# One level of Strassen's algorithm in the last stage of a hybrid encoder block

## The reference

```
n = rmsnorm(x, g1);  proj = n @ w_in              # 1024 -> 2048: q, k, v, u
att = rmsnorm(diff_attention(q, k, v), g_sub)     # 4 heads, width 512
ssm = bi_s5_glu(u)                                # width 512
h = x + concat(att, ssm) @ w_out                  # 1024 x 1024
h = h + square(relu(rmsnorm(h, g2) @ w_mlp1)) @ w_mlp2   # 1024 -> 4096 -> 1024
y = rmsnorm(h, g_final)
```

## Time and profile before

| | us |
|---|---|
| median of 3 runs | 2963.97 (2961.86 to 2968.33) |
| the profiled execution | 2968.97 |
| its span, first to last instruction | 2967.4 |
| PE busy / DVE busy / ACT busy / POOL busy | 2770.5 / 1709.1 / 1207.5 / 360.5 |
| matmuls on PE | 13768 |
| DMA | 322.47 MB, mean 109 GB/s |
| `phase_mlp`, its first instruction to the end | 1309.9 to 2967.4 |

### The profile page before, as it was taken

One profiled execution on the slowest core, in us unless ns is written; L12 is line 12 of the kernel. 1 busy time (PEld: TensorE's weight loads), 2 busy tenths in 40 slices (PEclk: granted clock), 3 DMA queues, 4 the chain that ended last, 5 costly groups with the idle time before them and its releaser, 6 DMA issues.

```text
span 2967.4 us, 37703 instructions
## 1 busy us (share of the span) xinstructions
PE 2770.5 (93%) x13768; PEld 2331.9 (79%) x13768; DVE 1709.1 (58%) x2380; ACT 1207.5 (41%) x1864; POOL 360.5 (12%) x300
## 2 busy tenths in 40 slices
PE   6978796999999979879999999999999999999996
PEld 5756585999999967767888878888788888788885
DVE  7665517999999947755434365343554343743434
ACT  3365514878787732233324223233233242332331
POOL 5220001101010013303000131000230001400001
PEclk9989898999999989989999999999999999999998
DMA  5335524020220049734232334322252322332222
GB/s 168 139 144 204 182 73 112 22 65 24 65 72 22 17 125 268 189 142 145 96 99 93 98 101 164 99 93 99 91 173 92 99 92 99 100 125 93 99 93 70
DMA packets 160986, 322.47 MB, mean 109 GB/s; under 512 B 30160, under 2 KB 87760, under 8 KB 157136
## 3 DMA queue, kind: packets, MB, share of 16 engines
q1 hardware_dynamic: 143568, 265.58, 29.1%
q10 hardware_dynamic: 10368, 29.89, 2.7%
q0 software_dynamic: 6912, 25.17, 2.3%
HBM read 255.05 MB, written 63.44 MB: 107 GB/s over the span
## 4 chain that ended last, share of the span: by engine, by line
PE 49%; DVE 3%; DMA 1%; issue 1%; POOL 0%; ACT 0%; DVEq 0%; POOLq 0%; ACTq 0%
PE ml_work L2130 9%; PE ml_work L2131 8%; PE ml_work L2132 8%; PE ml_down L2130 8%; PE ml_down L2132 8%; PE ml_down L2131 8%; DMA ml_x_in<-in_x_t 1%; DVE ml_w_lo L1805 1%; PE ml_spread L2093 0%; DVE ml_hg_lo L1946 0%; DVE ml_h L1942 0%; DVE ml_h_out L1931 0%; DMA ml_mix<-att_s 0%; DVE ml_h_out L2017 0%; DVE ml_square L2028 0%
## 5 line engine op out<-in xcount | busy, mean ns | idle before, releaser
L1805 DVE TENSOR_TENSOR ml_w_lo<-ml_w_raw,ml_w_hi 128x1024 fp32r<-128x1024 f32 x288 | 368.4, 1279 | 795.5 <-ACT ml_w_hi L1801 795.3
L1801 ACT ACTIVATE ml_w_hi<-ml_w_raw 128x1024 fp32r<-128x1024 f32 x288 | 305.5, 1061 | 1032.9 <-PE ml_down L2132 542.0
L2130 PE MATMUL ml_work<-ml_hg_hi,ml_w_hi 128*128 128x512 f32 x1024 | 399.4, 390 | 0.8 <-DVE ml_w_lo L1805 0.6
L2130 PE MATMUL ml_down<-ml_act_hi,ml_w_hi 128*128 128x512 f32 x1024 | 399.0, 390 | 0.0
L2132 PE MATMUL ml_work<-ml_hg_hi,ml_w_lo 128*128 128x512 f32 x1024 | 398.5, 389 | 0.0
L2132 PE MATMUL ml_down<-ml_act_hi,ml_w_lo 128*128 128x512 f32 x1024 | 398.4, 389 | 0.0
L2131 PE MATMUL ml_work<-ml_hg_lo,ml_w_hi 128*128 128x512 f32 x1024 | 398.4, 389 | 0.0
L2131 PE MATMUL ml_down<-ml_act_lo,ml_w_hi 128*128 128x512 f32 x1024 | 398.4, 389 | 0.0
L886 ACT ACTIVATE at_e<-at_e,at_neg_top 128x2048 f32<-128x2048 f32 x128 | 256.6, 2005 | 38.1 <-DVE at_neg_top L971 38.1
L1081 PEld LDWEIGHTS at_pv<-at_v,at_a_t 128*128 128x128 f32 x2048 | 259.0, 192 | 16.4
L1081 PE MATMUL at_pv<-at_v,at_a_t 128*128 128x128 f32 x2048 | 260.3, 276 | 0.0
(11 more groups left out here) (221 smaller groups left out, 4409.5 us busy)
## 6 DMA issues: line engine op xcount, KB each, us to landing
ml_w_raw<-in_w_stream SPq DMA_DIRECT2D x290, 512.0 KB, 3.5
tab_s<-pj_tab ACTq DMA_DIRECT2D x32, 512.0 KB, 2.6
pj_x_raw<-in_x_t SPq DMA_DIRECT2D x14, 1024.0 KB, 8.2
ss_tab<-tab_s SPq DMA_DIRECT2D x17, 512.0 KB, 13.7
pj_w_raw<-in_w_in SPq DMA_DIRECT2D x16, 512.0 KB, 4.0
qk_s<-pj_qku_out SPq DMA_DIRECT2D x32, 256.0 KB, 2.5
at_k_raw<-qk_s SPq DMA_DIRECT2D x16, 512.0 KB, 7.5
at_q_raw<-qk_s SPq DMA_DIRECT2D x128, 64.0 KB, 2.4
```

What stands on the lines that cost most here:

```text
L1801: act.activation(w_hi[:, r % 2], w_raw[:, (r + 2) % RAW], ACT.Copy).then_inc(w_hi_ready, 1)
L1805: dve.tensor_tensor(w_lo[:, r % 2], w_raw[:, (r + 2) % RAW], w_hi[:, r % 2].bitcast(F32), ALU.subtract)\
L2130: pe.matmul(out, lhs_hi, rhs_hi, start=first, stop=False)
```

## The change

`phase_mlp` is written anew. Each matrix product of 1024x1024 weights with 1024x1024 activations (a chunk) is split into 2x2 quarters of 512x512 and computed by Winograd's form of Strassen's algorithm: seven products of quarters (steps) instead of eight, with four sums of weight quarters (S1 to S4) and four of activation quarters (T1 to T4). There are 18 chunks: `MIX` for the two halves of 1024 tokens, then for each half four `UP` and four `DOWN`. A step is 4 output tiles (`slot`) by 4 k-tiles by the same three matmuls of 128x512. A quarter lies in a tile of 128x2048, so every split, sum and evacuation is one instruction of 2048 columns.

Two PSUM tiles of four banks alternate from step to step. The products that several results share are summed in PSUM: step 0's tile is copied to the other (`copy_over`, ACT, a quarter at a time), and later steps add to what a tile holds. After steps 1 to 6 the tile is added to a result `res` by DVE (`leave`), or in UP after steps 1, 2, 3 and 6 taken by ACT, which also applies Relu and Square. The split of step g+1 is made while step g is computed; DVE first evacuates step g-1.

Weights and activations are loaded by SP in quarters of 1 MB (`load_r`, `load_q`), the activations from memory: the relu-squares of UP (`act_s`), h (`h_s`) and the normalized h (`hn_s`) are stored there, from ACT's queue (`store_res`) and SP's. When h or y of a half is complete (after chunks 0, 1, 9 and 17; `event`), POOL sums its squares (`add_squares`, 14 adds), PE sums them over partitions with a matrix of ones (`statistics`, 128x512), ACT takes the root, DVE inverts 128x512 twice (`invert`) and multiplies 16 tiles of 128x512 (`normalize`), which SP reads back into two buffers `hb` and stores (`load_hb`, `store_hb`), during steps 0 to 4 of the next chunk. After the last chunk this is done at once, out of `res`.

The scaling and transposing of attention's output move into the gate loop of `phase_ssm`, one head's tile per item, two items behind: `att_scale` (DVE), `turn_att` (PE), `att_back` (ACT), `store_att` (SP). The 4 MB are loaded after `y_done`.

```diff
 # phase_ssm
+            sp.wait_ge(y_done, NGR)
+            for i in range(2):
+                for tb in range(2 * i, 2 * i + 2):
+                    sp.dma_start(att_in[:, tb], att_s.rearrange("h p t -> p h t")[:, :, tb * TB:(tb + 1) * TB])\
+                        .then_inc(att_loaded[i], 16)
...
+            def att_back(n):
+                act.wait_ge(att_turned, n + 1)
+                wait(act, att_stored[n % 2], 16 * (n // 2))
+                act.activation(att_out[:, n % 2], turn_ps[:, n % 2], ACT.Copy, scale=gain_att[:, 0:1]).then_inc(att_ready, 1)
...
+            act.wait_ge(total_step, 1)
+            act.activation(total[:], total[:], ACT.Sqrt).then_inc(total_step, 1)
...
+            def att_scale(n):
+                tb, c = n // H, n % H
+                if n in (0, 2 * H):
+                    dve.wait_ge(att_loaded[tb // 2], 32)
+                rows = att_in[:, tb, c].rearrange("p (c e) -> p c e", c=NC)
+                dve.tensor_tensor(rows, rows, total[:, c, tb * NC:(tb + 1) * NC].unsqueeze(2).to_broadcast([P, NC, P]),
+                                  ALU.mult).then_inc(att_scaled, 1)
...
+                for c in range(NC):
+                    last = pe.transpose(turn_ps[:, n % 2, c * P:(c + 1) * P], att_in[:, n // H, n % H, c * P:(c + 1) * P], ident[:])
+                last.then_inc(att_turned, 1)
             pe.wait_ge(glu_loaded, 32)
...
 # phase_mlp
-def phase_mlp(nc, x_t, att_s, att_square, att_floor, ssm_s, w_stream, gains, y_t):
...
+def phase_mlp(nc, x_t, att_t, ssm_s, h_s, hn_s, act_s, w_stream, gains, y_t, hb_stored):
...
+    MIX, UP, DOWN = 0, 1, 2
+    CHUNKS = [(MIX, 0, 0), (MIX, 1, 0)]
+    for s_ in range(2):
+        CHUNKS += [(UP, s_, c) for c in range(4)] + [(DOWN, s_, c) for c in range(4)]
...
+    SUM_OF = (None, C11, C12, C22, C22, C12, C21)
+    RESULTS = (C11, C22, C12, C21)
+    LAST_STEP = {C11: 1, C12: 5, C22: 4, C21: 6}
+    SQUARES = (C11, C22, C12, C21)
...
+    def by_act(k, i):
+        return kind(k) == UP and i in (1, 2, 3, 6)
...
+            def load_hb(e, n):
+                k = [k for k in EVENT if EVENT[k] == e][0]
+                s, reg, d = CHUNKS[k][1], TILES[n // 2], 2 * (n % 2)
+                sp.wait_ge(res_stored[reg], 16 * STORE_NO[k])
+                wait(sp, hb_stored[n % 2], 16 * (4 * e + n // 2))
+                sp.dma_start(hb[:, n % 2], h_s[s, reg].rearrange("p (d t) -> p d t", d=4)[:, d:d + 2]).then_inc(hb_loaded[n % 2], 16)
...
+            sp.dma_start(gain[:], gains).then_inc(consts_ready, 16)
+            load_r(0, R11)
+            load_q(0, Q11)
+            load_r(0, R12)
+            load_q(0, Q21)
+            load_q(0, Q12)
+            load_q(0, Q22)
+            load_r(0, R21)
+            load_r(0, R22)
...
+                    if i == 2 and following:
+                        load_r(k + 1, R22)
+                        if not late:
+                            load_q(k + 1, Q11)
+                    if i == 3 and following:
+                        load_r(k + 1, R11)
+                    if i == 4 and following:
+                        load_q(k + 1, Q12)
+                        load_r(k + 1, R21)
+                    if i == 5 and following:
+                        load_q(k + 1, Q22)
+                        load_r(k + 1, R12)
+                        if late:
+                            load_q(k + 1, Q11)
+                    if i == 6 and following:
...
+                        if i == 1:
+                            load_res(k, C12)
+                            load_res(k, C22)
+                        if i == 3:
+                            load_res(k, C21)
...
+                    pool.wait_ge(squared, squared_by(e, reg, d))
+                    wait(pool, added, done)
+                    pool.tensor_tensor(sums[:, t], sums[:, t], square[:, done % 2], ALU.add).then_inc(added, 1)
...
+        def raw_b(k, i):
+            return (q[Q11], q[Q21], q[Q11], t_first, q[Q12], q[Q22], q[Q21])[i]
+        def raw_w(k, i):
+            return (r[R11], r[R12], r[R11], s_first, r[R21], r[R12], r22[k % 2])[i]
...
+            def split_high_b(g):
+                k, i = g // STEPS, g % STEPS
+                wait(act, slot_done, 4 * (g - 1))
+                if i in (0, 1, 5):
+                    act.wait_ge(q_loaded[{0: Q11, 1: Q21, 5: Q22}[i]], 16 * (k + 1))
+                else:
+                    act.wait_ge(t_ready, 4 * k + {2: T2, 3: T1, 4: T3, 6: T4}[i])
...
+            def copy_over(k, d):
+                if d == 0 and k:
+                    evacuated(act, k - 1, 6)
+                act.wait_ge(slot_done, 4 * k * STEPS + d + 1)
+                act.activation(bank(k, 1)[:, d], bank(k, 0)[:, d], ACT.Copy).then_inc(copied, 1)
...
+                if g + 1 < NSTEP:
+                    split_high_b(g + 1)
+                    split_high_w(g + 1)
+                if k and keeps(k - 1) and i < 2:
+                    store_res(k - 1, C21 if i else C12)
+                if k + 1 < NCH and keeps(k) and i in (3, 6):
+                    store_res(k, C22 if i == 6 else C11)
+                if g and pi and by_act(pk, pi):
+                    leave(pk, pi)
+                if g and kind(pk) == UP and pi in (4, 5):
+                    finish(pk, pi)
+                if i == 0:
+                    copy_over(k, 0)
+                    copy_over(k, 1)
+                    if event is not None:
+                        rms(event, 0, bank(k, 0)[:, 3])
+                    copy_over(k, 2)
+                    copy_over(k, 3)
+                if event is not None:
+                    if i == 1:
+                        squares(k - 1, C21)
+                    if i == 3:
+                        rms(event, 1, bank(k, 3)[:, 3])
+                if whole(k):
+                    if i == 2:
+                        squares(k, C11)
...
+            def split_low_b(g):
+                k, i = g // STEPS, g % STEPS
+                dve.wait_ge(b_hi_ready, g + 1)
+                dve.tensor_tensor(b_split[:, g % 2, 1], raw_b(k, i)[:], b_split[:, g % 2, 0].bitcast(F32), ALU.subtract)\
+                    .then_inc(b_lo_ready, 1)
...
+            def sum_s1(k):
+                dve.wait_ge(r_loaded[R21], 16 * (k + 1))
+                dve.wait_ge(r22_loaded[k % 2], 16 * (k // 2 + 1))
+                if k:
+                    dve.wait_ge(w_lo_ready, (k - 1) * STEPS + 3 + 1)
+                dve.tensor_tensor(s_first[:], r[R21][:], r22[k % 2][:], ALU.add).then_inc(s_ready, 1)
...
+                dve.tensor_tensor(flat(res[reg]), flat(bank(k, i)), flat(res[reg]), ALU.add).then_inc(dve_left, 1)
+            def invert(e, n):
+                dve.wait_ge(rms_ready, 2 * e + n + 1)
+                dve.reciprocal(rinv[:, 1 - n], rinv[:, 1 - n]).then_inc(rinv_ready, 1)
...
+                dve.scalar_tensor_tensor(tile, tile, gain[:, at:at + 1], rinv[:, t], ALU.mult, ALU.mult).then_inc(norm_ready, 1)
...
+            split_low_b(0)
+            split_low_w(0)
+            sum_t1(0)
+            sum_t2(0)
+            sum_s1(0)
+            sum_s3(0)
...
+                if g and pi and not by_act(pk, pi):
+                    leave(pk, pi)
+                if g + 1 < NSTEP:
+                    split_low_b(g + 1)
+                    split_low_w(g + 1)
+                if i == 0:
+                    sum_s2(k)
+                if i == 1:
+                    sum_t3(k)
+                    sum_t4(k)
+                if i == 2:
+                    sum_s4(k)
+                if following:
+                    if i == 5 and not late:
+                        sum_t1(k + 1)
+                    if i == 5:
+                        sum_s1(k + 1)
+                    if i == 6 and late:
+                        sum_t1(k + 1)
+                    if i == 6:
+                        sum_t2(k + 1)
+                        sum_s3(k + 1)
+                if event is not None:
+                    if i == 1:
+                        invert(event, 0)
+                    if i == 3:
+                        invert(event, 1)
+                    if i in (1, 2, 3, 4):
+                        for n in range(4 * i - 4, 4 * i):
+                            if n % 2 == 0:
+                                dve.wait_ge(hb_loaded[n // 2 % 2], 16 * (4 * event + n // 4 + 1))
+                            normalize(event, n, hb[:, n // 2 % 2, n % 2], KD if kind(k - 1) == DOWN else 0)
...
+            def slot(k, i, d):
+                g = k * STEPS + i
+                if d == 0:
+                    pe.wait_ge(b_lo_ready, g + 1)
+                    pe.wait_ge(w_lo_ready, g + 1)
+                    if i >= 3:
+                        evacuated(pe, k, i - 2)
+                    elif i == 0 and k:
+                        evacuated(pe, k - 1, 5)
+                if i == 1:
+                    pe.wait_ge(copied, 4 * k + d + 1)
+                w_hi, w_lo = w_split[:, g % 2, 0], w_split[:, g % 2, 1]
```

(13 more changed lines are left out.)

976 lines of the change are left out of this document (445 added, 531 removed).

## The result

The changed kernel took 2781.3 us (median of 4 runs, 2778.5 to 2783.6) against 2963.1 for the kernel before beside it: ratio 0.938, 95% interval 0.937 to 0.940. The forecast was 2796.4, in a range from 2750 to 2858. The profiled execution took 2779.9 us with a span of 2778.1; before it was 2969.0 and 2967.4, so the two traces stand 189.1 us apart and the medians 182.

The account below looks back on a forecast made before the run. PE's matmul stream was taken to bound the last stage: 15 + 1370.9 + 3 + 10 + 4 + 47 + 29 = 1478.9 us against 1657.5; with +11 in `phase_ssm`, 167.6 off the median 2963.97 gave 2796.4, range 2750 to 2858.

Parts of the forecast that it names:

- fewer matmuls at the same spacing: Last stage: 6048 matmuls instead of 6912, still 226.7 ns apart, 1370.9 us, 195.8 less than before.
- VectorE keeps pace: Plain chunks: DVE needs 65.2 us in MIX and DOWN, 55.9 in UP, against 76.2 of PE.
- DVE sets the pace everywhere: Rival: at 2.85 us per DVE instruction a MIX or DOWN chunk takes 79.8 us; 2847 us in all; chance 0.20.
- the slower rival: Every DVE instruction takes 3.36 us, so MIX and DOWN chunks take 94.1 and UP 80.6; 3020 us; chance 0.05.
- Events: 47 and 4 forecast: Chunks around a finished h or y: PE waits 42 us plus 5 for round trips; statistics matmuls and their waits 4.
- The 3 us each for the own squares: Last two steps of chunks 0, 9 and 17, with two sums or none and seven adds: 3 us each.
- round trips and loads: Rival: `hb` rounds under 1 MB loads cost 10 us in each of three events, 15 in chunk 1; 2831; chance 0.10.
- Waits fit into slack: Rival: DVE's spare time absorbs overruns, so event waits are 10 us instead of 47, the start 5; 2754; chance 0.20.
- Start: 13 forecast: Chunk 0: PE waits 8 us behind DVE's sums and loads, its clock falls for 2 more, cold clock 3.
- Tail: 29 forecast: End of last stage: evacuation 2.3, two reciprocals 6.7, 16 normalizations 11.8, four contended adds 4.2, a store; about 29 us.
- `phase_ssm`: 11 forecast: Attention work moved into the gate loop: transposes 7 us, last item 2.5, square root 1.5; +11, bounds 3 and 22.
- DMA: nothing forecast: Last stage's loads and stores cost nothing, bounds 0 to 15 us; chunk 1 at 245 GB/s of 366.

Follow-up runs that it names:

- the moved sums: DVE makes step 1's splits in chunk 0 before that chunk's sums, against the changed kernel; 2778.6 us, ratio 0.936.
- short normalizations alone: Normalizations work on 16 of 512 columns in all four events, against the changed kernel; 2779.2 us, ratio 0.937.
- with the loads cut as well: Normalizations of 16 columns and six of eight pieces of h not read back, against the changed kernel; 2753.3 us, ratio 0.928.

## Why the prediction was right, and where it was off

The step that carried it, fewer matmuls at the same spacing, came out to the last digit: 6048 matmuls, 1370.9 us. It rested on the earlier trace rows rather than on a duration, and that is why it held: the records are still 0.39 long and the spacing still 226.7 ns. Of the figures that the Trainium skill has for this in "TensorE: Matmul & The Clock Gate", section "Back-to-back issue gap" (about 216 ns isolated, 131 sustained), neither is this kernel's spacing of 226.7.

*VectorE keeps pace: right.* 28 instructions in a DOWN chunk cost 61.6 us and not 65.2, since the spacing is 2.20 and I took 2.33; in a plain UP chunk it is busy for 0.70, below the 0.75 that I gave as the least. The fourteen plain chunks have no gap at all, which rules out "DVE sets the pace everywhere" (80 us a DOWN chunk) and the slower rival (94). What met an add took 3.38, close to the 3.36 of the earlier trace rows; that row was the rival's whole support, and it was a contended one, as argued.

*Events: 47 and 4 forecast, 43.4 measured, and nearly none of its parts right.* By chunk: 1 was put at 22 and was 15.9; 10 was put at 6 and was 10.7; 2 was put at 5 and was 16.8. For chunk 1 I had charged VectorE for each of 14 adds; nine of its instructions met one. With those nine at 1.1 and the measured spacings (2.20, 3.26 for a reciprocal, 0.66 for a normalization) the same sum gives 88.6 and not 98.4, that is 12 over 76.2. Chunk 2 is the step of the forecast that failed: it counted VectorE's instructions and found room for them. It saw that an add could take 3.4 us, but put the statistics at 1 to 2 us late per event; the whole chain of load, splits, squares, four adds of 3.2 us and statistics held the first step up by 8.1 in chunk 2, and by 3.4 and 2.8 in chunks 1 and 10. The 3 us each for the own squares of chunks 0, 9 and 17 were nothing in 9 and 17 (seven adds lengthened five VectorE instructions in chunk 9, 5.5 us, which its spare time hides, and none in chunk 17), and no step of chunk 0 behind the start is over 10.88. The 5 for round trips and 4 for statistics lie inside the three chunks. So the parts were off by -6, +12, +5, -9 and -9, in all -8: the sum is right by luck as much as by working. By cause, the loads of `hb` were worth 13.3 in steps 4-6 and not 5, and the normalizations' length was worth only 1.8 in the three chunks while those loads stood behind it. The rival "round trips and loads" named a true cause but put it on top of my 47, and it took the place of a part of them.

*"Waits fit into slack"* was half true: own squares did, events didn't.

*Start: 13 forecast, 8.9 measured,* cause confirmed by the moved sums. The first `s_first` started at 23.8 us into the stage and VectorE was done with step 1's splits at 32.8, where I had 25 and 34, and the clock cost 3.2 us and not the 5 of the forecast. The first matmul came 14.7 us in, near the 15 forecast; that this was "as now" was a slip, since the kernel before took 16.3.

*Tail: 29 forecast, 24.7 measured.* I had charged VectorE 4.2 us for four adds; two of them ran beside the reciprocal, which they don't lengthen, and the two others lengthened two normalizations. With the normalizations 0.66 apart and not 0.74, all sixteen took 12.8 us where 16.0 was forecast. The chain's rows (start, us, what), with 2.7 us left for the last store:

```profile
2753.55 2.29 DVE ml_res L2179
2755.84 3.27 DVE ml_rinv L2184
...
2759.89 6.73 DVE ml_res L2192 x7
2766.62 3.27 DVE ml_rinv L2184
...
2771.40 3.98 DVE ml_res L2192 x6
```

*`phase_ssm`: 11 forecast, 8 measured.* The gate loop's items are 3.24 us apart now, as forecast (3.2), against 2.80 in the earlier trace rows:

```profile
1291.20 0.69 ACT L1455 ACTIVATE sm_gate<-sm_y_ps,sm_bg 128x512 f32<-128x512 f32 x1 [1.97 <-PE sm_y_ps L1641]
...
1294.44 0.69 ACT L1455 ACTIVATE sm_gate<-sm_y_ps,sm_bg 128x512 f32<-128x512 f32 x1 [1.97 <-PE sm_y_ps L1641]
```

16 x 0.44 = 7.0 of the 8.0. Since this stage varies by up to 8 us between traces of the same code, the last 1 or 4 us can't be told apart, and no run took the att work out alone.

*DMA: nothing forecast, with 0 to 15 as bounds.* 251 GB/s in chunk 1 is what was forecast (245), and plain chunks wait for no load. But the latency of the `hb` loads and of Q11 is on the path in events, so "nothing" holds for throughput only.

The 15 us by which 2796 was too high are the tail (4), `phase_ssm` (3), chunk 0 (4), the events (8), together 19, and 2 ahead of the stages, less 7 us because the profiled execution of before lay 5 above its median and that of after 1.5 below.

## What to carry to other kernels

Take the pace from the distance of starts in a long uninterrupted stretch; it gave the large term exactly. At the places where an extra job meets a full engine, counting that engine's instructions isn't enough: follow the chain of small dependent pieces across engines (load, split, square, add, matmul), and price each link contended. And if cutting one suspect gives nothing, cut two: short normalizations alone gave 2 us, with the loads cut as well they gave 12.

## What the runs showed of the hardware

A VectorE instruction with both inputs in SBUF that meets a POOL add of 512 columns loses about the same 1.1 us whether it is 512, 1024 or 2048 wide (1.77 for 0.74, 2.31 for 1.21, 3.38 for 2.28), while the add itself waits longer the wider that instruction is (2.1 us beside halves of 1024, 3.2 beside 2048, 1.3 alone). A reciprocal, with one input, lost nothing beside an add (3.34 us, and 3.35 without adds). So the cost of the adds goes by how many of them meet an instruction with two inputs: 29 of 56 here, and 42 with instructions of half the width, in a kernel that was 20 us slower. And adding on VectorE itself (0.75 us each, 42 us for all) took more of its time than having POOL do it (29 x 1.1 = 32 us), and gained nothing.
